# Hybrid streaming encoder layer on one core: the experts' slot lists written by indirect scatters during attention

## The reference

```python
def hierarchical_moe(h, w_rg, w_re, w_g, w_u, w_d):
    lg = (h @ w_rg).astype(jnp.float32)
    p_group = jax.nn.softmax(lg, axis=-1)
    g_idx = jnp.argmax(lg, axis=-1)
    p_sel = jnp.take_along_axis(p_group, g_idx[:, None], axis=1)[:, 0]
    ...
    top_v, top_i = lax.top_k(le, TOP_K)
    combine = p_sel[:, None] * jax.nn.softmax(top_v, axis=-1)
    expert_id = g_idx[:, None] * EXPERTS_PER_GROUP + top_i
    ...
    def expert_block(args):
        xe, e = args
        return (jax.nn.silu(xe @ w_g[e]) * (xe @ w_u[e])) @ w_d[e]

def trunk_layer(...):
    ...
    x = x + jnp.concatenate([c, o], axis=-1) @ w_out
    h2 = rms_norm(x, norm_ffn_g).reshape(B * S, D_MODEL)
    x = x + hierarchical_moe(h2, ...).reshape(B, S, D_MODEL)
```

## Time and profile before

| | us |
|---|---|
| median of 3 runs | 2202.96 |
| lowest and highest | 2202.63, 2206.08 |
| the profiled execution | 2202.57 |
| its span | 2200.8 |

### The profile page before, as it was taken

One profiled execution on the slowest core, in us unless ns is written; L12 is line 12 of the kernel. 1 busy time (PEld: TensorE's weight loads), 2 busy tenths in 40 slices (PEclk: granted clock), 3 DMA queues, 4 the chain that ended last, 5 costly groups with the idle time before them and its releaser, 6 DMA issues. The chain is left out here.

```text
span 2200.8 us, 40164 instructions
## 1 busy us (share of the span) xinstructions
PE 2088.1 (95%) x13505; PEld 1771.5 (80%) x13506; DVE 1623.4 (74%) x2083; ACT 1260.0 (57%) x2200; POOL 806.9 (37%) x689
## 2 busy tenths in 40 slices
PE   8999999995899999899999895999999999999998
PEld 6888888884687887678787774888888888888887
DVE  3799999984777667867878967969698556556644
ACT  5322433335677777866676643768588555456533
POOL 1111544553566654545545435222222222222221
PEclk9999999996999999999999996999999999999999
DMA  7553344334333242333222117989899968767852
GB/s 228 186 191 134 118 128 159 120 106 144 114 117 109 80 131 81 108 105 116 80 73 92 54 70 258 361 281 372 308 357 373 329 197 282 228 198 264 285 172 35
DMA packets 211517, 393.17 MB, mean 179 GB/s; under 512 B 54749, under 2 KB 81757, under 8 KB 211389
## 3 DMA queue, kind: packets, MB, share of 16 engines
q1 hardware_dynamic: 197853, 357.42, 47.1%
q0 software_dynamic: 13536, 34.12, 6.8%
HBM read 315.42 MB, written 91.23 MB: 185 GB/s over the span
## 5 line engine op out<-in xcount | busy, mean ns | idle before, releaser
L2428 DVE TENSOR_TENSOR p_w_lo<-p_raw,p_w_hi 128x1024 fp32r<-128x1024 f32 (+1 forms) x260 | 439.5, 1728 | 150.5 <-ACT p_w_hi L2223 149.9
L2051 POOL TENSOR_TENSOR p_wgt<-p_wgt,p_past 128x1024 f32<-128x1024 f32 (+4 forms) x166 | 308.5, 1859 | 347.2 <-DVE p_past L1929 347.1
L2223 ACT ACTIVATE p_w_hi<-p_raw 128x2048 fp32r<-128x2048 f32 (+1 forms) x198 | 361.8, 1859 | 84.0 <-PE p_up L2310 67.3
L762 DVE SCALAR_TENSOR_TENSOR p_ut<-p_ut,p_cw 128x512 f32<-128x512 f32 (+1 forms) x480 | 329.2, 762 | 0.0
L1929 DVE TENSOR_TENSOR_SCAN p_past<-p_keep,p_past,p_one 128x513 f32<-128x513 f32 (+1 forms) x196 | 225.9, 1193 | 75.3 <-ACT p_keep L1746 73.3
L1746 ACT ACTIVATE p_keep<-p_zp 128x512 f32<-128x512 f32 (+3 forms) x326 | 158.8, 547 | 119.2 <-PE p_zp L1620 106.5
L2310 PE MATMUL p_gp<-p_w_hi,p_xt_hi 128*128 128x256 f32 x736 | 210.4, 286 | 0.0
L436 PE MATMUL p_pj<-p_w_hi,p_xt_hi 128*128 128x512 f32 x512 | 205.2, 401 | 4.2 <-DVE p_xt_lo L738 2.4
L2310 PE MATMUL p_gp<-p_w_lo,p_xt_hi 128*128 128x256 f32 x736 | 206.5, 281 | 0.0
L2310 PE MATMUL p_gp<-p_w_hi,p_xt_lo 128*128 128x256 f32 x736 | 206.4, 280 | 0.0
L436 PE MATMUL p_pj<-p_w_hi,p_xt_lo 128*128 128x512 f32 x512 | 200.6, 392 | 0.0
(11 more groups left out here) (309 smaller groups left out, 4975.6 us busy)
## 6 DMA issues: line engine op xcount, KB each, us to landing
p_raw<-in_w_up SPq DMA_DIRECT2D x128, 512.0 KB
p_raw<-in_w_gate SPq DMA_DIRECT2D x128, 512.0 KB
p_raw<-in_w_down SPq DMA_DIRECT2D x128, 512.0 KB
wide_raw<-in_w_in SPq DMA_DIRECT2D x56, 256.0 KB, 3.8
...
```

The costliest lines, as they stand in the source:

```text
L762: dve.scalar_tensor_tensor(dst, src, cw[:, a, j:j + 1], dst, ALU.mult, ALU.add).then_inc(tap_done, 1)
L2051: pool.tensor_tensor(mine, mine, past_rows[:, u % NP, 0:n, 2:2 + w], ALU.mult).then_inc(a_done, 1)
L2223: act.activation(part(w_hi, p, wide), raw[:, n % RING:n % RING + wide, :], ACT.Copy).then_inc(whi_done, wide)
L2428: dve.tensor_tensor(part(w_lo, p, wide), raw[:, n % RING:n % RING + wide, :], part(w_hi, p, wide).bitcast(F32), ALU.subtract).then_inc(wlo ...
```

## The change

The slots are no longer made from one-hot matrices. A DRAM array `lists` holds, for each expert, 17 regions of 128 entries (token, weight), and is zeroed at the start of attention, along with the tail rows of scr_h2 and y_out (7 stores from the zeros of q_dec). Once a batch is ranked, VectorE works out each choice's place (expert x 17 x 128 + rank) and weight, for which GpSimd raises e to the logits (`powers`), and GpSimd scatters token and weight there, one indirect DMA for each tile and choice (`scatter`, 34 in all, 128 rows of 8 bytes, 32 for the stream's tile). The scatters of a batch stand two to a step behind `product`. The expert stage gathers the 67 regions that hold blocks (67 rows of 1 KB), transposes them into PSUM, and two VectorE operations make the slots. ScalarE splits five pieces of weights, then the first tokens, then the other seven.

```diff
+REGION = NT
+LISTS = 768
+PAD = NT * P
...
-        self.expert = t[:, 0:2 * NT].rearrange("p (k t) -> p k t", k=2)
-        self.rank = t[:, 2 * NT:4 * NT].rearrange("p (k t) -> p k t", k=2)
-        self.second = t[:, 4 * NT:5 * NT]
-        self.group = t[:, 5 * NT:9 * NT].rearrange("p (t g) -> p t g", g=NG)
-        self.count = t[:, 9 * NT:9 * NT + NE]
+    def __init__(self, t, scattered):
+        self.count = t[:, 0:NE]
+        self.scattered = scattered
...
+        rank_step = {b: where["rank", b] for b in range(len(BATCHES))}
+        scatter_step = {}
+        for b in rank_step:
+            mine = [n for n, x in enumerate(choices) if x[0] == b]
+            scatter_step.update({n: min(rank_step[b] + 1 + x // 2, max(steps, rank_step[b] + 1)) for x, n in enumerate(mine)})
...
                 if t == PT:
                     sp.wait_ge(q_dec_zero, 1)
+                    sp.wait_ge(zero_in, 16 * 7)
...
+            def clear_lists():
+
+                zeros = q_dec[:, :, :, :].rearrange("p h a d -> p (h a d)")
+                sp.wait_ge(q_dec_zero, 1)
+                for n in range(3):
+                    part = scr["lists"][n * 256:(n + 1) * 256, :].rearrange("(p x) f -> p (x f)", x=2)
+                    sp.dma_start(part, zeros).then_inc(zero_in, 16)
+                for rows in (scr["h2"], io["y_out"]):
+                    for c in range(2):
+                        sp.dma_start(rows[PAD:ROWS, c * C:(c + 1) * C], zeros).then_inc(zero_in, 16)
...
+                if s == 0:
+                    clear_lists()
...
-                link(dve.tensor_tensor(picks.second[:, lo:hi], best[:, 3, 0:n], best[:, 2, 0:n], ALU.subtract))
+                links[0] += 1
+                dve.tensor_tensor(logit[:, 0:n, NG], best[:, 3, 0:n], best[:, 2, 0:n],
+                                  ALU.subtract).then_inc(logits_done, 1)
+                dve.sem_inc(picked, 1)
...
-                        mine = oh[k][:, 0:hi - lo, :]
-                        link(dve.tensor_tensor(mine, mine, cand[:, 0:hi - lo, :], ALU.mult))
-                        link(dve.tensor_reduce(picks.rank[:, k, lo:hi], mine, AX.X, ALU.add))
+                        mine = oh[k][:, 0:n, :]
+                        link(dve.tensor_tensor(mine, mine, cand[:, 0:n, :], ALU.mult))
+                        link(dve.tensor_reduce(rank[:, k, 0:n], mine, AX.X, ALU.add))
+                    if j[1]:
+                        dve.wait_ge(scattered, 16 * 2 * lo)
+                    link(dve.scalar_tensor_tensor(place[:, :, 0:n], expert[:, :, 0:n], float(REGION * P),
+                                                  rank[:, :, 0:n], ALU.mult, ALU.add))
+                    dve.wait_ge(powers_done, j[1] + 1)
+                    link(dve.tensor_reduce(total[:, 0, 0:n], power[:, 0:n, 0:NG], AX.X, ALU.add))
+                    link(dve.scalar_tensor_tensor(total[:, 1, 0:n], power[:, 0:n, NG], 1.0, total[:, 0, 0:n], ALU.add,
+                                                  ALU.mult))
+                    link(dve.reciprocal(entry[:, 0, lo:hi, 1], total[:, 1, 0:n]))
+                    link(dve.tensor_tensor(entry[:, 1, lo:hi, 1], entry[:, 0, lo:hi, 1], power[:, 0:n, NG], ALU.mult))
+                    dve.sem_inc(placed, 1)
...
+            def powers(b):
+
+                n = BATCHES[b][1] - BATCHES[b][0]
+                pool.wait_ge(logits_done, b + 1)
+                mine = logit[:, 0:n, :].rearrange("p t g -> p (t g)")
+                pool.tensor_tensor(power[:, 0:n, :].rearrange("p t g -> p (t g)"),
+                                   euler[:, 0:1].broadcast_to([P, n * (NG + 1)]), mine,
+                                   ALU.pow).then_inc(powers_done, 1)
+
+            def scatter(n):
+
+                b, c, r = choices[n]
+                x, rows = r - BATCHES[b][0], DEC if ORDER[r] == PT else P
+                pool.wait_ge(placed, b + 1)
+                if n == 0:
+                    pool.wait_ge(zero_in, 16 * 7)
+                pool.indirect_dma_start(out=scr["lists"].rearrange("r (s v) -> (r s) v", v=2),
+                                        out_offset=bass.IndirectOffsetOnAxis(ap=place[0:rows, c, x:x + 1], axis=0),
+                                        in_=entry[0:rows, c, r, :], in_offset=None).then_inc(scattered, 16)
...
                     product(s)
+                for b in at_step(pick_step, s - 2):
+                    powers(b)
+                for n in at_step(scatter_step, s):
+                    scatter(n)
...
-            sp.wait_ge(zero_yo, 1)
-            sp.dma_start(scr["h2"][PAD:ROWS, :], yo[:, :]).then_inc(zeroed, 16)
-            sp.dma_start(io["y_out"][PAD:ROWS, :], yo[:, :]).then_inc(zeroed, 16)
...
-            act.activation(gx[:, :, :], picks.group, ACT.Exp)
-            act.activation(ex[:, :], picks.second, ACT.Exp).then_inc(exped, 1)
-            act.activation(first[:, :], picks.second[:, 0:1], ACT.Silu)
+            act.activation(first[:, :], picks.count[:, 0:1], ACT.Silu)
...
+            lead((0, 0), 0, 5, 1)
+            x_hi(1)
+            lead((0, 0), 5, PIECES, 1)
             act.wait_ge(zero_yo, 1)
             act.sem_inc(yo_done, 1)
-            lead((0, 0), 0, PIECES, 1)
...
-            for n, (k, r) in enumerate(choices):
-                m = DEC if ORDER[r] == PT else P
-                if n in pool_rows:
-                    pe.wait_ge(row_in, pool_rows.index(n) + 1)
-                pe.wait_ge(spread_in, n + 1)
-                pe.matmul(up[:, 0:2 * NBL], homes[n % HOMES][0:m, :],
-                          in_col[0:m, n % RS, :, :].rearrange("p v b -> p (v b)"),
-                          start=(n == 0), stop=(n == len(choices) - 1)).then_inc(spread, 1)
+            pe.wait_ge(ident_done, 2)
+            pe.wait_ge(list_in, 16)
+            for v in range(2):
+                last = pe.transpose(up[:, v * NBL:(v + 1) * NBL], listed[:, :, v], ident[0:NBL, 0:NBL])
+            last.then_inc(list_ps, 1)
...
+            count, before, share = (nb[:, n, :] for n in range(3))
+            link(dve.tensor_scalar(count, picks.count, float(P - 1), None, ALU.add))
...
+            link(dve.tensor_tensor(before, before, count, ALU.subtract))
+            link(dve.tensor_scalar(share[:, 1:NE], count[:, 0:NE - 1], -1.0, float(REGION), ALU.mult, ALU.add))
+            dve.wait_ge(consts, 2)
+            link(dve.tensor_copy(row[:, :], row_i[:, :]))
+            link(dve.scalar_tensor_tensor(share, before, row[:, 0:1], share, ALU.is_le, ALU.mult))
+            link(dve.tensor_reduce(over[:, :], share, AX.X, ALU.add))
+            link(dve.tensor_scalar(over_i[:, :], over[:, :], row[:, 0:1], 0.0, ALU.add, ALU.max))
+            dve.sem_inc(region_done, 1)
+            link(dve.tensor_scalar(last_pad[:, :], row[:, :], 0.0, float(LISTS * P), ALU.is_ge, ALU.mult))
+            link(dve.tensor_scalar(last_pad[:, :], last_pad[:, :], float(PAD), None, ALU.add))
+            link(dve.tensor_scalar(table[0:1, 0, :], before[0:1, :], 1.0, None, ALU.add))
+            link(dve.tensor_tensor(table[0:1, 1, :], before[0:1, :], count[0:1, :], ALU.add))
             dve.sem_inc(table_done, 1)
-            tt(oh[:, :, :], iota[:, 0:NE].unsqueeze(1).broadcast_to([P, NC, NE]), over(flat(picks.expert), NE),
-               ALU.is_equal)
-            tt(oh[:, :, :], oh[:, :, :], nb[:, 1, :].unsqueeze(1).broadcast_to([P, NC, NE]), ALU.mult)
-            link(dve.tensor_reduce(sel[:, :], oh[:, :, :], AX.X, ALU.add))
-            tt(col[:, :], hi[:, :], sel[:, :], ALU.add)
-
-            dve.wait_ge(exped, 1)
-            link(dve.tensor_reduce(se[:, :], gx[:, :, :], AX.X, ALU.add))
-            link(dve.scalar_tensor_tensor(den[:, :], ex[:, :], 1.0, se[:, :], ALU.add, ALU.mult))
-            link(dve.tensor_copy(tok[:, :], tok_i[:, :]))
-            link(dve.tensor_copy(pad[:, :], pad_i[:, :]))
-            for k in range(2):
-                tt(vw[:, k * NT:(k + 1) * NT, 0], tok[:, :], row[:, k * NT:(k + 1) * NT], ALU.subtract)
-            link(dve.reciprocal(vw[:, 0:NT, 1], den[:, :]))
-            tt(vw[:, NT:NC, 1], vw[:, 0:NT, 1], ex[:, :], ALU.mult)
-
-            for n in range(NC):
-                if n >= RS:
-                    dve.wait_ge(spread, n - RS + 1)
-                if n not in pool_rows:
-                    dve.tensor_scalar(homes[n % HOMES], iota[:, :], row[:, n:n + 1], None, ALU.is_equal)
-                dve.scalar_tensor_tensor(in_col[:, n % RS, :, :],
-                                         iota[:, 0:NBL].unsqueeze(1).broadcast_to([P, 2, NBL]), col[:, n:n + 1],
-                                         vw[:, n, :].unsqueeze(2).broadcast_to([P, 2, NBL]), ALU.is_equal,
-                                         ALU.mult).then_inc(spread_in, 1)
-
-            dve.wait_ge(spread, NC)
-            link(dve.tensor_scalar(slot_f[:, :], up[:, 0:NBL], pad[:, 0:1], None, ALU.add))
+
+            dve.wait_ge(list_ps, 1)
```

(17 more changed lines are left out.)

113 lines of the change are left out of this document (43 added, 70 removed).

## The result

The changed kernel takes 2222.88 us (median of 4 runs, 2221.87 to 2224.37), beside 2202.8 us for the kernel before on the same chip: a ratio of 1.009, 95% interval 1.0075 to 1.0105. I had predicted 2204 with a range up to 2221. The side was the likeliest of my three (slower, 0.49), but my case said "no change", and the time lies just above the range.

The account below looks back on a forecast made before the run. Expert blocks were taken as rigid, PE alone, so only the first expert matmul's shift counted: tail +14.8, experts' start -15.9, attention +2.5, sum +1.4 us on 2202.57, giving 2204 us, range 2198 to 2221.

Parts of the forecast that it names:

- my case: Whole kernel: tail's loss and experts' gain nearly cancel, 2204 us, own range 2199 to 2209; chance 0.38.
- Blocks rigid: Expert stage: 46 blocks stay at 17.86 us each; only the first expert matmul shifts.
- Step 1: Tail of attention: power of 15 logits ahead of the last inverse RMS takes 3.0 us, VectorE's rows 3.8 later.
- Step 2: Tail of attention: five new linked VectorE operations at 0.22 us each, 1.1 us, hidden for batch 3.
- Step 3: Tail of attention: batch 3's six scatters at 1.1 us each on GpSimd, four ahead of batch 4's power.
- rival (b): Tail and attention: a scatter costs GpSimd 2.0 us, like the accumulating one; +9.6 us, 2214; chance 0.19.
- Step 4: Tail of attention: VectorE waits some 4.6 us before batch 4's places for 30 scatters to land, 3.5 us landing.
- Step 5: End of attention: four last scatters, then 1.39 us as before to the expert stage's start, 14.8 us later in all.
- landing 4.2 us: Start of the experts: 67-row list gather lands in 4.2 us, between 3.5 and 6.9, having a quarter of the bytes.
- rival (a): Start of the experts: the 67 list rows come through one DMA engine; +7 us, 2211; chance 0.2.
- the warming matmuls: Start of the experts: 22 warming matmuls at 0.41 us, 9.1 us, set the token transposes, not the gather.
- Within attention: Batches 0 to 2 and start of attention: powers, scatters, VectorE operations +2 us (0 to +8), stores +0.5.

Follow-up runs that it names:

- e6: Changed kernel without the drain of GpSimd at the end of the attention stage; 2220.28 us.
- e1: Changed kernel with the list gather taking 80 rows instead of 67; 2219.27 us.
- e11: Changed kernel with the list gather taking 68 rows instead of 67; 2217.81 us in one run.
- e2: Changed kernel with a GpSimd addition of the same shape in place of each power, true weights left out; 2212.44 us.
- e3: Changed kernel without the 34 scatters, semaphore only counted up, lists left empty; 2207.45 us.
- e5: Changed kernel without four of the five linked VectorE operations for batches 0 to 2; 2218.46 us.
- e9: Changed kernel with 80-row gather, places tile per batch, no drain, ScalarE sigmoids for powers; batches 0 to 2's places and weights two to three steps later; 2203.35 us.
- e10: e9 with the first tokens gathered from one loaded list row, by mistake an empty one, so the first block's tokens were left out; 2199.39 us.
- e13: e10 with the right list row (17) and batch 2's places and weights no longer delayed; 2195.55 us, 0.996 of the kernel before.
- e7: Changed kernel with two ScalarE sigmoids instead of GpSimd powers, six linked VectorE operations instead of five; 2211.73 us.
- e12: The kernel before, unchanged, run once more for a second trace; 2204.21 us.

## Why the prediction was wrong, by its steps

**Blocks rigid.** Right: 17.89 us in after, and in the second trace of before too.

**Step 1, the power of 15.** Right: 2.75 us for 3.0, VectorE's rows 3.6 us later for 3.8. **Step 2**, five linked operations, 1.0 us for 1.1. **Step 3**, a scatter at 1.1: 0.96 to 1.07 with a pitch of 1.26; rival (b) was wrong. A scatter started 0.35 us behind VectorE's release and not 0.85. The power of 10: 1.98 for 2.1. **Step 4**, the wait for the landing: right in place, 4.06 us for 4.6, landing 2.6 for 3.5, between the small store's 1.7 and my value. The Trainium skill, page DMA: Bandwidth & Descriptors, section on the anatomy of one DMA on the GpSimd path, has a fixed price of about 2.0 us; the 2.6 measured lies closer to that than mine.

**Step 5, the end of the stage.** Here the tail's miss lies. I took over 1.39 us from VectorE's last operation to T0. But the change put four DMAs of GpSimd at the very end, and GpSimd's drain waits for them: 4.01 us from the last scatter's end, 0.96 without the drain (e6). A fixed cost read from before was fixed only as long as no DMA of that engine was in flight.

**The start of the experts.** The term "landing 4.2 us" failed. It was 10.95 to the transposes. 4.6 of the excess is rival (a), the one engine, which I had given a fifth (with (b), three tenths) though the rule cited with it spoke for it and no row against it; e1 and e11 show it. My +7 for it was too high, and that hid a second error: spread over the engines the gather takes 6.2, close to the 6.9 of the 4 KB rows that I had as the upper bound. My step "a quarter of the bytes", and so nearer the lower end, has no support: beside the weight loads (DMA share 1.00 in after's stretch below) 4.5 of e1's 6.2 us pass ahead of the gather's first packet and 1.0 in moving the bytes. The window from T0 to the first expert matmul, after:

```profile
1358.56:1387.13 28.57, 10.78 (x41) 8.20 (x41) 11.71 (x25) 9.39 (x10) 7.47 (x12) 0.64 1.00 361
```

Also, the warming matmuls did not bind: 7.35 us for the 22, 0.33 each and not 0.41, and the transposes waited 1.5 us for the tokens. My 4.35 us from the transposes to the first expert matmul were those of one execution at the lower clock: 3.77 in after, 3.75 in the second trace of before.

**Within attention**, the largest miss: 11.0 us by the last batches where I took 2.5 (9.0 against the second trace of before). The step that failed is its argument, not one number. I compared GpSimd's new work with its idle time, and held VectorE "late now and then". In fact:
- A power that stands ahead of a product does not use GpSimd's idle time, which lies elsewhere. I had put the product behind batch 0's power 2.2 us later, "into a pipeline of three units"; the pipeline took up none of it. Batch 0's power cost 2.4 us, batch 1's 1.3, batch 2's nothing (e2).
- The scatters, on which most of my upper bound rested, cost nothing (e3).
- VectorE's five operations stand in the one step of each batch in which everybody waits for VectorE: 1.0 to 1.1 us in full for batches 0 and 1 (e2 against before; e5, e9), and 1.0 for batch 2 against the second trace of before.
- Behind them TensorE had idled 3.7 us, for 1.7 before, and got a lower clock, 0.84 and 0.77 for 1.00: another 1.6 to 2.3 us after batch 0, and in one trace of two 1.5 at batch 1. With the operations moved (e9, e10, e13) the clock stayed at 1.00; one trace with them in place (e7) kept it too.

Together 8.5 to 10.7 us, by trace. The 1.6 us by which the changed kernel's trace was late at scan 240, ahead of all this, are the execution's.

**The sum.** 8.5 of the 16.8 us missed are attention, 6.3 the experts' start, 2.1 the tail. (The other 2 us up to the median are the block microsecond and the profiled execution, which is 1.0 us below the median.) What I had right (each new operation's own duration) was not where the time went; it went where they stood.

What stays open: why the clock's dips in attention fall now here and now there between two executions of one kernel. In e13 they cost nothing until scan 280 and 1.3 us at 316, as in e12.
